# Weights laid out in memory by eight keys: whole rows for the loads, 512-byte pieces for the stores

## The chip, the core and the metric

The kernel runs on one core of a Trainium2 chip. The metric is the time of one execution on the device, in microseconds, as the median of several runs. One further execution was profiled; every duration below comes from it.

## What is computed

One inference step of a small trunk layer: modulation, latent attention and retention in parallel, an output projection, and then an expert layer (PEER) on 9 tiles of 128 tokens. Only the expert layer matters here. Each token picks 16 of 16384 experts for each of 8 heads, an expert being a pair of keys (i, j) with i and j below 128:

```python
eidx = jnp.take_along_axis(cidx, sel, axis=-1)
g = jax.nn.softmax(top_s, axis=-1).astype(xb.dtype)
act = jax.nn.gelu(jnp.einsum('thkd,td->thk', u_table[eidx], xb), approximate=False)
return jnp.einsum('thk,thkd->td', g * act, v_table[eidx])
```

## The kernel before

The first three tiles of tokens (the sparse ones) gather their experts' rows. The other six are done densely, in two groups of 384 tokens: for each of the 128 values of key j, TensorE multiplies the tokens by all 128 experts (i, j) of `u` (lines 2835, 2836 and 2839, in high and low halves, into `p_a`), ScalarE applies gelu, VectorE multiplies by the token's weight for that expert (line 2689, `w_ring`), and TensorE multiplies by the experts of `v` into `p_y` (line 2853). One value of j is a step.

The weights of a group are a tensor over 128 i (the partitions), 128 j and 384 tokens. Class `WeightSteps` makes them, four tokens at a time: VectorE writes one-hot rows (`vector`), TensorE multiplies them (`tensor`, line 2252), ScalarE copies the product from its bank to `wt` (`scalar`, line 2260). Four such calls fill a block of 16 tokens, of which `wt` holds two, and `store` (lines 2262 to 2267) writes a block, 1 MB, to `w_dram` in memory ("weights_spill" in the rows). The store first waits for every store before it (line 2265 counts it), then frees a half of `wt` for ScalarE, then waits for ScalarE's four copies, then issues.

The work is written out by hand for each engine, and each engine and each queue runs its list in order:

- The first group's 24 blocks are made ahead of the steps, in a stage of their own. SyncE stores them, and issues between two stores a load of `u_ahead` (buffers named `rows<-in_uT` in the rows), of `hs` (`x1g<-h_spill`) or of the first u and v. TensorE meanwhile multiplies ahead for the last 16 steps (line 2810, `down_ahead`) and ScalarE sends the results to memory (`act_ahead`).
- The second group's 24 blocks are made during steps 0 to 95 of the first group, one block every four steps; GpSimd stores them.
- The weights come back by eight keys j and all 384 tokens, 1.5 MB at a time, into one of the two halves of `w_ring` (`load_w`, line 2574, issued by GpSimd once every eight steps). The very first is loaded in four parts while the last blocks are still being made (line 2601).
- Behind these on GpSimd's queue stand the gathers of the sparse tiles (line 2583, 768 of 512 KB), whose rows VectorE uses between its other work (lines 2702 and 2714).

In memory a block was `[128 i, 128 j, 16 tokens]`, so that a store wrote 8 KB in one piece per row, and a load of eight keys read 24 pieces of 512 bytes per row, one from each block, 1 MB apart.

Of the kernel before, what the change touches and what calls it, by code (L numbers as in the profile page):

```python
# [6 lines left out]
F32 = mybir.dt.float32  # L7
# [9 lines left out]
P = 128  # L17
# [20 lines left out]
N_KEYS = 128  # L38
N_EXPERTS = N_KEYS * N_KEYS
GROUP = 3  # L40
SPARSE = 3
DENSE_AT = SPARSE * P
DENSE = T - DENSE_AT
BLOCK = 16
NEG = -3.0e38
SHARE_UNIT = 2.0 ** 14
LATE_PIECES = 16
# [1229 lines left out]
def wait_count(eng, sem, count):  # L1277

    if not isinstance(count, int) or count > 0:
        eng.wait_ge(sem, count)  # L1280
# [380 lines left out]
def stage_scores(nc, sem, m, keep, a):  # L1661
# [71 lines left out]
    with nc.Block() as block:  # L1733
# [328 lines left out]
        def _(dve):  # L2062
# [77 lines left out]
            def sixteen_best(x, rest, values, where, groups):  # L2140
# [7 lines left out]
                for g in groups:  # L2148
                    last = nc.vector.match_replace(rest[:, g, :], values[:, g, 0:8], x[:, g, :], NEG)
                link(last)  # L2150
# [51 lines left out]
class WeightSteps:  # L2202
# [7 lines left out]
    STEPS = GROUP * P // B  # L2210
    PER_BLOCK = BLOCK // B
    LEAD = 2

    def __init__(self, nc, sem, m, keep, iota):
# [6 lines left out]
        self.iota = iota.rearrange("p (k b) -> p k b", b=self.IN)  # L2221
        self.wt = m.sb("wt", [P, 2, N_KEYS, BLOCK])
        self.iota_full, self.equal_full, self.hot_full, self.pw_full, self.pw_read, self.wt_free, self.stored, self.stored_next = (
# [38 lines left out]
    def store(self, eng, block, stored, ahead=0):  # L2262

        wait_count(eng, stored, (block - ahead) * 16)
        eng.sem_inc(self.wt_free, 1)
        eng.wait_ge(self.pw_read, block * self.PER_BLOCK + (self.PER_BLOCK + self.LEAD))
        eng.dma_start(self.keep.w_dram[block], self.wt[:, block % 2]).then_inc(stored, 16)


def stage_experts(nc, sem, m, keep, a):  # L2270
# [15 lines left out]
    x1 = [m.sb(f"x1g{i}", [P, D]) for i in range(GROUP)]  # L2286
    w = WeightSteps(nc, sem, m, keep, keep.pairsT[:, 2, DENSE_AT:DENSE_AT + N_KEYS * WeightSteps.IN // 2].bitcast(F16))
    BLOCKS = w.STEPS // w.PER_BLOCK
    JC = 8
    TB = GT // BLOCK  # L2290
    w_ring = m.sb("w_ring", [P, 2, TB, JC, BLOCK])
    rows = [[m.sb(f"rows{s}{i}", [P, D]) for i in range(SLOTS)] for s in range(SPARSE)]
# [31 lines left out]
    h_in, u_in, v_in, w_in, w_early = sem("h_in"), pair("u_in"), pair("v_in"), sem("w_load"), sem("w_early")  # L2324
# [11 lines left out]
    def out_rows(t):  # L2336
        return a["out"][0][0] if t == 0 else a["out"][1][0, (t - 1) * P:t * P, :]
# [21 lines left out]
    def parts_after(g, j):  # L2359

        whole = J - AHEAD * g
        total = J + 2 * whole
        passed = j + 1 + 2 * min(j + 1, whole)
        return min(SPARSE * J, -(-SPARSE * J * passed // total) + SPARSE * ((j >= 4) + (j >= 8)))
# [56 lines left out]
    with nc.Block() as block:  # L2421
# [143 lines left out]
        @block.gpsimd  # L2565
        def _(pool):
            CHUNKS = J // JC

            def load_w(g, c):

                n = c + g * CHUNKS
                wait_count(pool, w_in, n * 16)
                wait_count(pool, g_full, (n - 1) * JC + 1)
                pool.dma_start(w_ring[:, n % 2], keep.w_dram[g * TB:(g + 1) * TB, :, c * JC:(c + 1) * JC, :].rearrange("b i j t -> i b j t")).then_inc(w_in, 16)

            def gather(g, j, paced=lambda s: None):

                n = g * J + j
                for s in range(SPARSE):
                    paced(s)  # L2580
                    wait_count(pool, rows_used, (n - SLOTS) * SPARSE + s + 1)
                    at = bass.IndirectOffsetOnAxis(ap=keep.experts[:, s, j:j + 1].bitcast(U32), axis=0)
                    pool.indirect_dma_start(rows[s][n % SLOTS][:], None, (keep.u_rows, v_rows)[g], at).then_inc(rows_in[s][n % SLOTS], 16)  # L2583

            def load_x1(g):
                for i in range(GROUP):
                    wait_count(pool, y_out[0][i], 16 * g)
                    pool.dma_start(x1[i][:], keep.x1_dram[SPARSE + g * GROUP + i]).then_inc(x1_in[i], 16)

            pool.dma_start(h_ahead, keep.h2_dram[:, :, DENSE_AT + GT:DENSE_AT + 2 * GT]).then_inc(h_ahead_in, 16)  # L2590
            for i, part in enumerate(H_PARTS):
                pool.wait_ge(w.stored, 16 * (H_BEHIND + i))
                wait_count(pool, h_in, 16 * i)
                pool.dma_start(h_lo[:, part, :].bitcast(F32), keep.h2_dram[:, part, DENSE_AT:DENSE_AT + GT]).then_inc(h_in, 16)
            pool.wait_ge(idx_done, 2)
            for g in range(GROUPS):
                if g == 0:
                    gather(g, 0, lambda s: pool.wait_ge(w.stored, 16 * (ROWS_BEHIND + s)))
                    for blocks_in, behind in W_BEHIND:
                        pool.wait_ge(w.stored, 16 * behind)  # L2600
                        pool.dma_start(w_ring[:, 0, blocks_in], keep.w_dram[blocks_in, :, 0:JC, :].rearrange("b i j t -> i b j t")).then_inc(w_in if behind == BLOCKS else w_early, 16)
                    pool.wait_ge(ahead_full, STEPPED)
                    gather(g, 1)
                else:
                    gather(g, 0)
                    gather(g, 1)
                    load_w(g, 0)
                load_w(g, 1)
                if g == 0:
                    pool.wait_ge(cols_turned, SPARSE)  # L2610
                    load_x1(0)
                asked = SLOTS
                for j in range(J):
                    enough = min(parts_after(g, j) // SPARSE + SLOTS, J)
                    for n in range(asked, enough):
                        gather(g, n)
                    asked = max(asked, enough)
                    if g < GROUPS - 1 and j < w.STEPS and j % w.PER_BLOCK == w.PER_BLOCK - 1:
                        w.store(pool, j // w.PER_BLOCK + BLOCKS, w.stored_next, BLOCKS)
                    if j % JC == JC - 1 and j // JC + 2 < CHUNKS:  # L2620
                        load_w(g, j // JC + 2)
                    if g == 0 and j == w.STEPS + 8:
                        pool.wait_ge(w.stored_next, 16 * BLOCKS)
                        pool.dma_start(h_next, keep.h2_dram[:, :, DENSE_AT + GT:DENSE_AT + 2 * GT]).then_inc(h_in, 16)
                    if g and j == 4:
                        for i in range(GROUP):
                            pool.wait_ge(y_full, i + 1)
                            pool.dma_start(out_rows(SPARSE + i), x1[i][:]).then_inc(y_out[0][i], 16)
                    if g and j == 16:
                        load_x1(1)  # L2630
            for s in range(SPARSE):
                pool.wait_ge(rows_used, (2 * J - 2) * SPARSE + s + 1)
                pool.dma_start(x1_sparse[s], keep.x1_dram[s]).then_inc(xs_in[s], 16)

        @block.vector
        def _(dve):
# [43 lines left out]
            def weigh(n, j, s):  # L2680
# [6 lines left out]
                dve.wait_ge(w_in, (n // JC) * 16 + 16)  # L2687
                three = lambda x: x.rearrange("p (b t) -> p b t", t=BLOCK)
                nc.vector.tensor_mul(three(g_all[s]), three(act_g[s]), w_ring[:, (n // JC) % 2, :, n % JC, :]).then_inc(g_full, 1)  # L2689
# [194 lines left out]
def build(nc, a, debug=None):  # L2884
    with ExitStack() as stack:
        top = Mem(nc, stack)
        keep = Keep()
# [23 lines left out]
        keep.z_dram = nc.dram_tensor("z_spill", [TILES, P, Z_RET], F32).ap()  # L2911
        keep.x1_dram = nc.dram_tensor("x1_spill", [TILES, P, D], F32).ap()
        keep.h2_dram = nc.dram_tensor("h2_spill", [P, KD, T], F32).ap()
        keep.w_dram = nc.dram_tensor("weights_spill", [DENSE // BLOCK, P, N_KEYS, BLOCK], F32).ap()
        keep.u_rows = nc.dram_tensor("u_rows", [N_EXPERTS, D], F32).ap()
        keep.w_in_in = [stack.enter_context(nc.semaphore(f"w_in_in{c}")) for c in range(2)]

# [52 lines left out]
        keep.h_rows = top.sb("h_rows", [P, SPARSE, D])  # L2970
        keep.index, keep.parts = (top.sb(x, [P, 2, DENSE], F16)[:] for x in ("index", "parts"))
        run(stage_experts)


# [41 lines left out]
```

## Time and profile before

| | |
|---|---|
| median of 3 runs | 3575.25 us |
| the runs | 3573.58, 3575.25, 3584.92 us |
| the profiled execution's own time | 3585.65 us |
| its span, first to last instruction | 3583.9 us |
| TensorE busy | 3444.2 us, 96% |
| VectorE busy | 2941.8 us, 82% |
| ScalarE busy | 1391.3 us, 39% |
| GpSimd busy | 1483.9 us, 41% |
| moved by DMA | 1047.91 MB, mean 292 GB/s |

The busy shares are means over stages with different limits; the stage with the first group's weights is 137 us of the 3584, the steps about 2100. A DMA's time to landing runs from its issue to its last semaphore write. Rows name engines as PE (TensorE), DVE (VectorE), ACT (ScalarE), POOL (GpSimd) and SP (SyncE); a q behind the name is the engine's queue of instructions. The DMA engines serve three queues here: q1 is SyncE's, q10 ScalarE's, q0 GpSimd's.

### The profile page before, as it was taken

The page shows a single profiled execution, that of the slowest core. Times are in us where ns is not written, and L with a number is a line of the kernel's source. Part 1 is how long each engine was busy: PE and PEld are TensorE (multiplying, and loading weights), DVE is VectorE, ACT ScalarE, POOL GpSimd, SP SyncE. Part 2 cuts the span into 40 slices and gives each one's busy share as a digit, 9 for nine tenths or more (in the row PEclk, how much of TensorE's full clock was granted, in tenths as well). Part 3 has the DMA queues.
Part 4 walks back from the last instruction along what each step waited for, and adds up shares of the span by engine and source line. Part 5 has one row for each costly group of instructions (what it writes and reads, how often), then busy time and mean ns, then how long its engine had stood idle before and what let it go on. Part 6 is the DMA issues. An engine that isn't in the chain of part 4 may idle for free.

```text
span 3583.9 us, 55129 instructions
## 1 busy us (share of the span) xinstructions
PE 3444.2 (96%) x18146; PEld 2870.1 (80%) x18146; DVE 2941.8 (82%) x5762; ACT 1391.3 (39%) x2125; POOL 1483.9 (41%) x1121
## 2 busy tenths in 40 slices
PE   7899989988999989999999999999999999999998
PEld 2899869876444456788888998899988999999987
DVE  8455678854688899799999999988888988988988
ACT  7411464462122238434444444433333333333332
POOL 3233020052322210254444444454466776666761
PEclk9999999999999989999999999999999999999999
DMA  8599429856311138999999999999999999999997
GB/s 310 205 359 354 157 101 320 300 215 211 132 35 35 65 119 322 325 355 348 346 354 352 339 354 351 350 357 367 311 344 376 379 364 369 374 355 363 374 364 286
DMA packets 399666, 1047.91 MB, mean 292 GB/s; under 512 B 32106, under 2 KB 185550, under 8 KB 390194
## 3 DMA queue, kind: packets, MB, share of 16 engines
q0 software_dynamic: 134416, 505.99, 39.1%
q1 hardware_dynamic: 213612, 478.03, 36.6%
q10 hardware_dynamic: 51512, 62.42, 5.0%
q8 instruction: 53, 0.87, 0.1%
q14 instruction: 73, 0.60, 0.1%
HBM read 892.52 MB, written 153.80 MB: 292 GB/s over the span
## 4 chain that ended last, share of the span: by engine, by line
PE 55%; DMA 4%; DVE 2%; issue 1%; ACT 0%; POOL 0%; ACTq 0%; DVEq 0%; SPq 0%; POOLq 0%
PE p_y L2853 26%; PE p_a L2836 9%; PE p_a L2839 8%; PE p_a L2835 8%; PE pw L2252 1%; DMA weights_spill<-wt 1%; DMA pairsT<-act_ahead 1%; PE p_y L2810 1%; DMA rows<-in_v,pairsT 1%; DVE rows L2702 0%; DMA x1g<-h_spill 0%; DMA rows<-u_rows,pairsT 0%; DVE h_rows L2714 0%; POOL rows L2583 0%; ACT wt L2260 0%
## 5 line engine op out<-in xcount | busy, mean ns | idle before, releaser
L2583 POOL DMA_INDIRECT rows<-u_rows,pairsT x384 | 492.2, 1282 | 580.8 <-DVE pairsT L2702 531.9
L2583 POOL DMA_INDIRECT rows<-in_v,pairsT x384 | 591.6, 1541 | 333.2 <-DVE h_rows L2714 248.2
L2835 PE MATMUL p_a<-h_hi,u_hi 128*128 128x384 f32 x1856 | 624.0, 336 | 4.9 <-ACT pairsT L2531 4.0
L2836 PE MATMUL p_a<-h_lo,u_hi 128*128 128x384 f32 x1856 | 627.3, 338 | 0.0
L2714 DVE SCALAR_TENSOR_TENSOR h_rows<-rows,pairsT,h_rows 128x1024 f32<-128x1024 f32 x381 | 476.8, 1280 | 53.8 <-DMA rows<-in_v,pairsT 53.6
L2702 DVE CUSTOM_DVE_ANT_0 rows<-rows,h_rows 128x1024 f32<-128x1024 f32 x384 | 459.2, 1220 | 22.1 <-DMA rows<-u_rows,pairsT 22.0
L2853 PE MATMUL p_y<-v_hi,g_hi 128*128 128x512 f32 x1464 | 464.8, 399 | 4.7 <-ACT g_hi L2537 4.7
L2853 PE MATMUL p_y<-v_lo,g_hi 128*128 128x512 f32 x1464 | 454.6, 391 | 0.0
L2853 PE MATMUL p_y<-v_hi,g_lo 128*128 128x512 f32 x1464 | 373.2, 390 | 3.0 <-DVE g_lo L2696 3.0
L2839 PE MATMUL p_a<-h_hi,u_lo 128*128 128x384 f32 x1856 | 361.1, 335 | 8.3 <-DVE u_lo L2662 8.3
L2835 PEld LDWEIGHTS p_a<-h_hi,u_hi 128*128 128x128 f32 x1856 | 350.1, 189 | 15.4 <-issue 5.3
L2836 PEld LDWEIGHTS p_a<-h_lo,u_hi 128*128 128x128 f32 x1856 | 349.7, 188 | 8.9
L2537 ACT ACTIVATE g_hi<-pairsT 128x384 fp32r<-128x384 f32 x256 | 134.7, 526 | 568.3 <-DVE pairsT L2689 563.8
L2524 ACT ACTIVATE v_hi<-v_raw 128x1024 fp32r<-128x1024 f32 x244 | 257.4, 1055 | 243.9 <-PE p_y L2853 241.6
L2662 DVE TENSOR_TENSOR u_lo<-u_raw,u_hi 128x1024 fp32r<-128x1024 f32 x232 | 283.2, 1221 | 64.9 <-ACT u_hi L2506 64.9
L2839 PEld LDWEIGHTS p_a<-h_hi,u_lo 128*128 128x128 f32 x1856 | 325.9, 188 | 9.3 <-DVE u_lo L2662 9.2
L2853 PEld LDWEIGHTS p_y<-v_lo,g_hi 128*128 128x128 f32 x1464 | 275.1, 188 | 62.5
L2853 PEld LDWEIGHTS p_y<-v_hi,g_lo 128*128 128x128 f32 x1464 | 275.5, 188 | 60.6 <-DVE g_lo L2696 3.4
L2678 DVE TENSOR_TENSOR v_lo<-v_raw,v_hi 128x1024 fp32r<-128x1024 f32 x244 | 297.8, 1221 | 9.3 <-ACT v_hi L2524 6.4
L2853 PEld LDWEIGHTS p_y<-v_hi,g_hi 128*128 128x128 f32 x1464 | 265.6, 188 | 49.1 <-ACT g_hi L2537 6.4
L1904 PE MATMUL psc<-wc,hs 128*128 128x512 f32 x576 | 251.5, 595 | 0.0
L2260 ACT ACTIVATE wt<-pw 128x512 f32 (+1 forms) x144 | 157.3, 1092 | 237.7 <-PE pw L2252 223.8
(386 smaller groups left out, 6013.7 us busy)
## 6 DMA issues: line engine op xcount, KB each, us to landing
v_raw<-in_v SPq DMA_DIRECT2D x244, 512.0 KB, 6.6
u_raw<-in_uT SPq DMA_DIRECT2D x232, 512.0 KB, 7.3
w_ring<-weights_spill POOLq DMA_DIRECT2D x31, 1536.0 KB, 14.5
wada<-in_w_ada SPq DMA_DIRECT2D x48, 512.0 KB, 7.0
u_rows<-pairsT ACTq DMA_DIRECT2D x48, 512.0 KB, 6.8
key_cols<-in_uT SPq DMA_DIRECT2D x48, 512.0 KB, 7.5
u_rows<-key_rows SPq DMA_DIRECT2D x48, 512.0 KB, 5.7
weights_spill<-wt SPq DMA_DIRECT2D x24, 1024.0 KB, 5.1
```

What stands on the lines that cost most here:

```text
L1904: last = nc.tensor.matmul(psc[:, 4 * b:4 * b + 4, :], hs[:, k, :], wc[:, k, 4 * b:4 * b + 4, :], start=k == 0, stop=k == KD - 1)
L2260: self.nc.scalar.activation(out.rearrange("p j b -> p b j"), banks[s % len(banks)], ACT.Copy, scale=1.0 / SHARE_UNIT).then_inc(self.pw_rea ...
L2524: nc.scalar.activation(hi, raw, ACT.Copy).then_inc(vhi_full, 1)
L2583: pool.indirect_dma_start(rows[s][n % SLOTS][:], None, (keep.u_rows, v_rows)[g], at).then_inc(rows_in[s][n % SLOTS], 16)
L2662: nc.vector.tensor_sub(u_lo[s][:], u_raw[s][:], u_hi[s][:].bitcast(F32)).then_inc(ulo_full, 1)
L2678: nc.vector.tensor_sub(lo, raw, hi.bitcast(F32)).then_inc(vlo_full, 1)
L2702: nc.vector.tensor_tensor_reduce(out=slot[:], in0=slot[:], in1=keep.h_rows[:, s, :], op0=ALU.mult, op1=ALU.add, scale=1.0, scalar=0.0, acc ...
L2714: nc.vector.scalar_tensor_tensor(out=total, in0=slot[:], scalar=share, in1=total, op0=ALU.mult, op1=ALU.add).then_inc(rows_used, 1)
L2835: nc.tensor.matmul(p_a[:, 0:GT], u_hi[s][:, k, :], h_hi[:, k, :], start=k == 0, stop=False)
L2836: nc.tensor.matmul(p_a[:, 0:GT], u_hi[s][:, k, :], h_lo[:, k, :], start=False, stop=False)
L2839: last = nc.tensor.matmul(p_a[:, 0:GT], u_lo[s][:, k, :], h_hi[:, k, :], start=False, stop=k == KD - 1)
L2853: last = nc.tensor.matmul(p_y[i][:, half, :], part[s][:, i * P:(i + 1) * P], vv[:, half * 512:(half + 1) * 512], start=begin, stop=stop)
```

## The change

The tensor in memory gets another order: group, chunk of eight keys, i, block, key in the chunk, token. A store takes the same block from `wt` and writes it as 16 pieces of 512 bytes per row i, one for each chunk, 1.5 MB apart. A load of a chunk reads 12 KB in one piece per row; the four early parts read 4 KB or 2 KB in one piece per row. No instruction is added, removed or moved on any engine: only the shapes of the 48 stores and the 35 loads differ.

```diff
+W_KEYS = 8
...
-        eng.dma_start(self.keep.w_dram[block], self.wt[:, block % 2]).then_inc(stored, 16)
+        group, b = divmod(block, GROUP * P // BLOCK)
+        rows = self.keep.w_dram[group][:, :, b].rearrange("c i j t -> i c j t")
+        eng.dma_start(rows, self.wt[:, block % 2].rearrange("i (c j) t -> i c j t", j=W_KEYS)).then_inc(stored, 16)
...
-                pool.dma_start(w_ring[:, n % 2], keep.w_dram[g * TB:(g + 1) * TB, :, c * JC:(c + 1) * JC, :].rearrange("b i j t -> i b j t")).then_inc(w_in, 16)
+                pool.dma_start(w_ring[:, n % 2], keep.w_dram[g, c]).then_inc(w_in, 16)
...
-                        pool.dma_start(w_ring[:, 0, blocks_in], keep.w_dram[blocks_in, :, 0:JC, :].rearrange("b i j t -> i b j t")).then_inc(w_in if behind == BLOCKS else w_early, 16)
+                        pool.dma_start(w_ring[:, 0, blocks_in], keep.w_dram[0, 0][:, blocks_in]).then_inc(w_in if behind == BLOCKS else w_early, 16)
...
-        keep.w_dram = nc.dram_tensor("weights_spill", [DENSE // BLOCK, P, N_KEYS, BLOCK], F32).ap()
+        keep.w_dram = nc.dram_tensor("weights_spill", [DENSE // (GROUP * P), N_KEYS // W_KEYS, P, GROUP * P // BLOCK, W_KEYS, BLOCK], F32).ap()
```

## Rows read from the trace of the kernel before

**Rows 1.** Busy by stretch: us; PE, PEld, DVE, ACT, POOL (instructions); clock, DMA, GB/s.
```profile
1389.00:1442.00 53.00, 51.44 (x393) 33.31 (x392) 51.00 (x149) 42.76 (x49) 7.78 (x8) 1.00 0.98 355
...
1600.00:2345.00 745.00, 745.00 (x4218) 669.89 (x4217) 682.02 (x1181) 322.78 (x423) 339.99 (x288) 1.00 0.96 348
...
2620.00:3500.00 880.00, 867.52 (x4352) 785.52 (x4351) 783.55 (x789) 312.47 (x417) 590.03 (x382) 1.00 0.98 367
...
1577.00:1584.00 7.00, 6.41 (x20) 5.86 (x20) 5.94 (x12) 0.00 (x0) 4.82 (x3) 0.54 1.02 397
```

**Rows 2.** What SyncE's queue waited for, 1315 to 1475 us: total, times, longest.
```profile
SPq L2265 <- DMA weights_spill<-wt: 101.2, 23, 6.6
SPq L2267 <- ACT wt L2260: 23.6, 12, 13.3
```

**Rows 3.** The 24 stores on SyncE: issue in ns; then landing in us, min/median/max.
```profile
L2267 SPq DMA_DIRECT2D weights_spill<-wt x24: 319/326/332, 1326.8 to 1463.7; - x24
...
DMA to landing us min/median/max: 4.4/5.1/6.9
```

**Rows 4.** Chain that ended last, 1388 to 1443 us: start, us, what.
```profile
by line: DMA weights_spill<-wt 85.4%; ACT wt L2260 8.3%; issue 5.6%; ACT pairsT L2495 0.6%; ACTq L2497 0.6%; SPq L2265 0.3%; ACTq L1280 0.0%; ACTq L2258 0.0%
...
1406.81 5.19 DMA weights_spill<-wt
...
1412.09 6.93 DMA weights_spill<-wt
```

**Rows 5.** The tensor h_spill on SyncE's queue, 880 to 1240 us.
```profile
L1754 SPq DMA_DIRECT2D h_spill<-hs x9: 540/561/602, 888.9 to 1231.2; - x9
...
DMA to landing us min/median/max: 3.7/3.8/8.8
```

**Rows 6.** The tensor x_spill on SyncE's queue, the same stretch.
```profile
L1752 SPq DMA_DIRECT2D x_spill<-x x8: 350/352/371, 903.4 to 1214.5; - x8
...
DMA to landing us min/median/max: 2.6/2.7/2.7
```

**Rows 7.** DMA, 1103.3 to 1107 us; a queue's packets, MB, share of 16 engines.
```profile
DMA packets 1080, 0.69 MB, mean 186 GB/s; under 512 B 16, under 2 KB 1040, under 8 KB 1080
...
q1 hardware_dynamic: 1080, 0.69, 70.7%
```

**Rows 8.** DMA, 1326.8 to 1330.4 us; issues with KB and us to landing.
```profile
q1 hardware_dynamic: 121, 0.99, 82.9%
...
rows<-in_uT SPq DMA_DIRECT2D x1, 512.0 KB, 5.7
```

**Rows 9.** Between the weights' stage and the steps: timeline of POOL, then the chain.
```profile
1468.82 0.75 POOL L2601 DMA_DIRECT2D w_ring<-weights_spill  x1 [20.27 <-DMA weights_spill<-wt]
...
1469.53 7.12 DMA act_ahead<-pairsT
```

**Rows 10.** All DMA issues: KB each, median us to landing.
```profile
x1g<-h_spill SPq DMA_DIRECT2D x3, 512.0 KB, 7.2
...
w_ring<-weights_spill POOLq DMA_DIRECT2D x2, 256.0 KB, 6.7
```

**Rows 11.** DMA, 1482 to 1485.5 us, while a load of weights ran.
```profile
q0 software_dynamic: 240, 0.98, 99.3%
```

**Rows 12.** DMA, 1488.1 to 1489.9 us, while rows of 4 KB were loaded.
```profile
q0 software_dynamic: 194, 0.73, 101.1%
```

**Rows 13.** The tensor weights_spill: time of an issue on GpSimd, ns min/median/max.
```profile
L2574 POOL DMA_DIRECT2D w_ring<-weights_spill x31: 1455/1498/1512, 1475.6 to 3510.9; - x31
...
L2267 POOL DMA_DIRECT2D weights_spill<-wt x24: 579/592/607, 1521.1 to 2340.2; - x24
```

**Rows 14.** Who waited for whom, 2650 to 2720 us: total, times, longest.
```profile
DVE h_rows L2714 <- DMA rows<-in_v,pairsT: 9.6, 5, 5.4
...
PE p_a L2839 <- DVE u_lo L2662: 8.3, 2, 7.3
```

**Rows 15.** The same view, 1570 to 1590 us.
```profile
PE p_y L2853 <- DVE g_lo L2696: 3.0, 1, 3.0
```

More of the change, by code:

```diff
@@ L2288, in stage_experts @@
     BLOCKS = w.STEPS // w.PER_BLOCK
-    JC = 8
+    JC = W_KEYS
     TB = GT // BLOCK
```

## The prediction, made before the changed kernel ran

> **What bounds the kernel now.** I read the busy shares by stretch first, then what the store's queue waits for, then the chain that ended last, because the change touches only transfers and a transfer matters where something waits for it.
>
> The kernel writes and reads the weights in two very different places. From 1600 to 2345 us, the first group's steps, TensorE is busy 745.00 of 745.00 us, and from 2620 to 3500 us 867.52 of 880, while the DMA engines are 96% and 98% busy [rows 1]. There TensorE is the bound, and a transfer counts only where it makes TensorE wait. From about 1327 to 1464 us lies the stage that makes the first group's weights: 24 blocks, each stored by SyncE. Its middle, 1389 to 1442 us, shows TensorE 51.44, VectorE 51.00 of 53 us, and the DMA engines at 0.98 [rows 1]: three things are near their limit at once. The order of waits settles it. SyncE waited 101.2 us, 23 times, for the previous store to land, and 23.6 us for ScalarE to fill the next block; the longest of these, 13.3 us, is the wait ahead of the first store [rows 2]. So between the first store (1326.8) and the last (1463.7) only 23.6 - 13.3 = 10.3 us passed in which the data and not the previous store was late. The stores take 4.4 to 6.9 us to land, median 5.1 [rows 3]. The chain of work shows the same: from 1388 to 1443 us 85.4% of it is store after store, the next one issued 0.09 us after the one before has landed (1412.09 behind 1406.81 + 5.19) [rows 4]. The code says why: `store` waits for all earlier stores before it hands ScalarE the other half of `wt`, and one store is in flight at a time. This is the one place where a microsecond of a store is a microsecond of the kernel.
>
> **The stores of the first stage (the term that decides).** 23 intervals take 136.9 us; without the 10.3 us of slack they are 126.6 us, 5.50 us each: a landing and a restart. If a store lands d later, the stage needs 23 x (5.50 + d) us, which is 23d - 10.3 us more than now, and nothing below d = 0.45. Nothing hides it: ScalarE has two halves of `wt`, both then full or in flight, and TensorE and VectorE are let on by ScalarE's reads of the banks. Everything on SyncE's queue behind the store (the loads of `u_ahead`, which feed the matmuls ahead of the steps, and the first u and v) moves along.
>
> What is d? The trace holds a pair that differs only in pieces. `h_spill<-hs` writes 512 KB in 1024 pieces of 512 bytes and lands in 3.8 us; its issue takes 561 ns [rows 5]. `x_spill<-x` writes 512 KB in 128 pieces of 4 KB, lands in 2.7 us, and its issue takes 352 ns [rows 6]. So 1.1 us more for 1024 pieces. A second way goes by the packets: around one `h_spill` store 1080 packets ran, 1024 of them the pieces, 16 semaphore writes and 40 packets of the load behind it, and took 70.7% of 16 engines in 3.7 us [rows 7], 41.9 us; less 40 x 163 ns (below) that is 35 ns a piece. So SyncE's queue does not join pieces. A store of today is 8 KB packets, 121 in 82.9% of 16 x 3.6 us [rows 8], 395 ns each, or 25 ns per 512 bytes. The change makes 2048 pieces of each store: 2048 x 10 ns / 16 = 1.3 us, and the longer issue adds about 0.2. I take d = 1.5. The low end is the 1.1 us of the pair as it stands, the high end twice that, 2.2 us, since there are twice the pieces. So the stage grows by 24.2 us (15.0 to 40.3).
>
> The Trainium skill (DMA: Bandwidth & Descriptors, Specifications) puts the smallest piece at line rate at 512 bytes, by which d would be 0 and the term 0; the same page (Why small descriptors are slow) charges some 3 cycles on top of 16 for a 512-byte piece, 19%, which as an estimate on 3.2 us of packets is d = 0.6 and a term of 3.5 us. [Rows 7, 8] speak against both: 35 against 25 ns.
>
> **The end of that stage.** After the last store lands, GpSimd issues the last piece of the first weights (1468.82) [rows 9]; such a piece takes 6.7 us [rows 10], so it is there at about 1475.5, and ScalarE waits for another transfer, `act_ahead<-pairsT`, from 1469.53 for 7.12 us anyway [rows 9]. A store 1.5 us later uses up the 1.2 us of margin, and the piece, now 2 KB per row instead of four pieces, gives some back. I put 0, at most 1 us.
>
> **The loads of the steps.** 31 loads of 1.5 MB are now 24 pieces of 512 bytes per row and become one of 12 KB. GpSimd's queue joins pieces to 4 KB packets: while only a w load ran, 240 packets took 99.3% of 16 x 3.5 us, 232 ns each [rows 11]; while 4 KB rows ran, 0.73 MB, 178 packets, took 101.1% of 16 x 1.8 us, 163 ns each [rows 12]. A load is 384 packets, so it gives the engines 384 x 69 / 16 ns = 1.7 us back, and GpSimd's issue falls from 1498 ns to about the 592 ns that 128 pieces cost [rows 13]. A gather that is issued behind a load lands some 2.6 us sooner.
>
> The 24 stores on GpSimd go the other way: between 592 ns (128 pieces) and 1498 ns (3072) [rows 13] 2048 pieces lie at 1.2 us, and 256 packets at 232 ns are 3.7 us of the engines where 128 at 326 to 395 ns are 2.6 to 3.2. So each costs 0.6 us of issue and 0.5 to 1.1 us of transfer. Behind them wait gathers, behind these VectorE's dots, and behind these TensorE; in the stretch with 745 of 745 us of matmul nothing of it arrives [rows 1]. If that cover were gone it would be at most 24 x 1.7 = 41 us.
>
> What can be won is what TensorE waits today because of late gathers: 8.3 us around 2695, behind a VectorE that waited up to 5.4 us for rows of `in_v` [rows 14], and 3.0 us at 1577 [rows 15]. Behind the second the granted clock was 0.54 from 1577 to 1584, so near the lower of its two levels, 1.2 GHz [rows 1]. The first becomes 2.6 us shorter. The second has a store and a load ahead of its gathers: 2.6 less, 1.1 to 1.7 more, so 1.0 shorter. Together -3.6 us, with the clock's dip left.
>
> **Sum.** The profiled execution took 3585.65 us (span 3583.9, 1.75 around it). 3585.65 + 24.2 + 0 - 3.6 = 3606. It stands 10.4 us over the median of the runs, so the median becomes 3596 us. A measurement here tells about 0.3% (11 us) from no change.
>
> **Rivals.**
> (a) The small pieces cost little (d below 1.1): the store's 8 KB packets of today are already held up by memory, so shorter ones may fit into the same time. For it speaks 395 ns against 326 ns, twice the 4 KB packet; against it the pair of rows 5 and 6. At d = 0.45 or less it gives 3575.25 - 3.6 = 3572, at 0.7 3577. Chance 0.22 with all that ends within 0.3%.
> (b) The other side: faster. The gathers behind the shorter loads come soon enough that TensorE never waits in the steps. That is worth 8.3 + 3.0 us and the dip (7 us at 0.54, 3.2 us; twice that if the longer wait has one too), 18 us, and 3557 if the stores cost nothing. It decides only if the stage grows by less than 6 us, which is d below 0.7, and the profile's waits recur in the unprofiled runs. DMA at 98% in the steps speaks for it, TensorE at 867.5 of 880 for its small size. Chance 0.06.
> (c) Much slower. Small pieces suffer beside other traffic: `x1g<-h_spill`, 512 KB in 1024 pieces behind a store, lands in 7.2 us [rows 10], a load of 512 KB in 4 KB pieces behind a store in 5.7 [rows 8]: 1.5 us for 1024 pieces, d = 3.0 for 2048. The pieces of a row now lie 1.5 MB apart too. The stage grows by 58.7 us: 3630. TensorE, with 5.8 us of work per block (0.97 of today's 136.9 / 23 = 5.95), would then idle 2.7 us in 8.5, close to the 3.0 us that it had idled when the clock stood at 0.54. Chance 0.12.
> The forecast itself (d from 1.1 to 2.2; 3587 to 3612) has 0.60.
>
> **Numbers.** The range takes the forecast's own range, the upper part of (a) down to d = 0.7, and the lower part of (c): 3577 to 3616. Slower by over 0.3% (above 3586): 0.60 + 0.12. Within: 0.22. Faster: 0.06.
>
> **What would show it.** In the profile after, the 24 stores on SyncE land in a median of 6.4 to 6.8 us instead of 5.1 and their issue takes about 0.8 us; SyncE's wait for ScalarE between stores is nearly gone; from the first store to the last it is 160 us, not 137; TensorE's share in that stage falls from 0.97 to 0.83 with the clock still at 1. The w loads take about 0.6 us to issue and land some 2 us sooner. VectorE waits less for `in_v` rows. I am wrong if the stores land below 5.6 us, or if the stage grows and the steps shrink by as much, which needs TensorE waits that the trace of before doesn't have.

## The result, and the profile after

| | before | changed |
|---|---|---|
| median | 3581.41 us (7 runs) | 3594.84 us (7 runs) |
| range of the runs | 3573.58 to 3584.92 | 3590.25 to 3601.26 |
| ratio | | 1.004, 95% interval 1.0029 to 1.0051 |
| span of the profiled execution | 3583.9 us | 3593.4 us |
| first to last store of the first stage | 136.9 us | 157.5 us |
| last of these stores to the end | 2120.2 us | 2114.6 us |

The changed kernel is 0.4% slower. Between the two profiled executions there are 9.5 us: 20.6 more in the stage that makes the first group's weights, 5.6 less behind it, and 5.5 less ahead of the first store, where nothing was changed and executions simply differ.

What SyncE's queue waited for in that stage of the changed kernel, as in [rows 2]; lines have moved by three:

```profile
SPq L2266 <- DMA weights_spill<-wt: 90.2, 23, 9.2
SPq L2270 <- ACT wt L2261: 18.4, 7, 13.4
```

The stores on SyncE, as in [rows 3]:

```profile
L2270 SPq DMA_DIRECT2D weights_spill<-wt x24: 359/374/385, 1321.3 to 1478.8; - x24
...
DMA to landing us min/median/max: 5.3/5.8/9.6
```

The median landing has gone from 5.1 to 5.8 us and the longest from 6.9 to 9.6. The wait for ScalarE between stores (without the first one's 13.4) is 5.0 us where it was 10.3: the chain of stores sets nearly every interval. What a store costs without other traffic shows at the first one of the changed kernel. In the 5.2 us behind its issue (1321.3 to 1326.5) SyncE's queue moved

```profile
q1 hardware_dynamic: 2059, 1.08, 77.8%
```

That is 77.8% of 16 engines for 5.2 us, or 31 ns a packet, where 512 bytes of an 8 KB packet took 25 ns in [rows 8]. For 2048 pieces on 16 engines the difference is 0.8 us a store. The chain that ended last, 1380 to 1445 us, as in [rows 4]:

```profile
by line: DMA weights_spill<-wt 98.6%; PE p_y L2813 4.1%; ACT wt L2261 3.3%; PE p_a L2253 1.3%; issue 1.2%; PE pw L2253 1.0%; SPq L2266 0.2%; ACTq L2259 0.0%
...
1374.70 5.60 DMA weights_spill<-wt
...
1386.21 8.12 DMA weights_spill<-wt
...
1414.72 9.57 DMA weights_spill<-wt
...
1424.37 5.68 DMA weights_spill<-wt
...
1430.13 9.32 DMA weights_spill<-wt
```

The shares add up to more than 100%, since the first store of this chain begins at 1374.70, ahead of the stretch. Without it the stores are some 58.8 of the 65 us, 90%.

Busy times by stretch, the columns of [rows 1]. First the whole stage of the kernel before:

```profile
1326.80:1463.70 136.90, 131.80 (x998) 87.18 (x997) 127.26 (x364) 108.75 (x118) 9.47 (x10) 0.97 0.88 314
```

then of the changed kernel: that stage, a piece of it, and the second and third stretch of [rows 1], moved to where the same work now lies:

```profile
1321.30:1478.80 157.50, 140.06 (x1003) 91.38 (x1001) 129.76 (x365) 107.89 (x118) 7.53 (x10) 0.93 0.90 273
...
1424.00:1431.00 7.00, 5.49 (x29) 3.88 (x30) 2.86 (x8) 5.07 (x6) 1.72 (x2) 0.51 0.79 231
...
1613.00:2358.00 745.00, 745.00 (x4217) 669.92 (x4216) 682.24 (x1182) 323.07 (x423) 348.01 (x288) 1.00 0.95 349
...
2628.00:3509.00 881.00, 872.36 (x4373) 789.93 (x4372) 790.12 (x793) 315.18 (x419) 577.40 (x384) 1.00 0.97 369
```

In the stage TensorE has the same work and shows 8 us more of it, since its clock was at the lower level, 1.2 GHz, for part of the time: from 1424 to 1431 us the granted clock is 0.51, after TensorE had waited 3.6 us for ScalarE. The steps of the first group are as full of matmul as before, 745 of 745 us. In those of the second group TensorE's waits have shrunk, from 12.5 of 880 us (880 - 867.52) to 8.6 of 881. The part of [rows 13] and of [rows 14], after:

```profile
L2577 POOL DMA_DIRECT2D w_ring<-weights_spill x31: 561/592/612, 1491.4 to 3520.0; - x31
...
L2270 POOL DMA_DIRECT2D weights_spill<-wt x24: 1208/1229/1250, 1535.4 to 2352.8; - x24
```

```profile
DVE h_rows L2717 <- DMA rows<-in_v,pairsT: 8.6, 7, 3.4
...
PE p_a L2842 <- DVE u_lo L2665: 6.3, 2, 5.3
```

### The profile page after: what moved, and what is told of

Same layout as the page of the kernel before. It is cut to its first block, busy times and chain, and to the rows that moved or that the text cites. A ratio compares the mean times of both kernels' runs of the same rounds, so it can differ in the third digit from the quotient of the medians.

```text
span 3593.4 us, 55129 instructions
## 1 busy us (share of the span) xinstructions
PE 3445.0 (96%) x18146; PEld 2868.0 (80%) x18146; DVE 2947.2 (82%) x5762; ACT 1391.3 (39%) x2125; POOL 1465.6 (41%) x1121
## 4 chain that ended last, share of the span: by engine, by line
PE 54%; DMA 6%; DVE 2%; issue 1%; POOL 0%; ACT 0%; SPq 0%; DVEq 0%; ACTq 0%
PE p_y L2856 26%; PE p_a L2839 9%; PE p_a L2842 8%; PE p_a L2838 8%; DMA weights_spill<-wt 3%; PE pw L2253 1%; DMA pairsT<-act_ahead 1%; DMA rows<-in_v,pairsT 1%; PE p_y L2813 0%; DVE rows L2705 0%; DMA x1g<-h_spill 0%; POOL rows L2586 0%; DMA rows<-u_rows,pairsT 0%; DVE h_rows L2717 0%; DVE u_lo L2665 0%
## 5 line engine op out<-in xcount | busy, mean ns | idle before, releaser
L2705 DVE CUSTOM_DVE_ANT_0 rows<-rows,h_rows 128x1024 f32<-128x1024 f32 x384 | 458.8, 1220 | 10.3 <-DMA rows<-u_rows,pairsT 10.3
L2681 DVE TENSOR_TENSOR v_lo<-v_raw,v_hi 128x1024 fp32r<-128x1024 f32 x244 | 298.1, 1222 | 12.5 <-ACT v_hi L2527 7.0
## 6 DMA issues: line engine op xcount, KB each, us to landing
w_ring<-weights_spill POOLq DMA_DIRECT2D x31, 1536.0 KB, 11.8
```

Of the source, the lines that this page charges most:

```text
L2681: nc.vector.tensor_sub(lo, raw, hi.bitcast(F32)).then_inc(vlo_full, 1)
L2705: nc.vector.tensor_tensor_reduce(out=slot[:], in0=slot[:], in1=keep.h_rows[:, s, :], op0=ALU.mult, op1=ALU.add, scale=1.0, scalar=0.0, acc ...
```

## The experiments

My theory: the loss lies in SyncE's 24 stores of the first stage and there alone; it is the price of small pieces times a chain in which one store waits for the landing of the last; the loads of the steps give a few microseconds back. Rivals: GpSimd's small stores cost in the steps; the distance between the pieces and not their size matters; the DMA engines are simply full.

### Half of the change each (late_only, early_only)

```diff
+        if group == OLD_GROUP:
+            eng.dma_start(self.keep.w_blocks[b], self.wt[:, block % 2]).then_inc(stored, 16)
+            return
```

The group `OLD_GROUP` keeps the order of before, in a tensor of its own, and its loads are those of before: group 0 in late_only, group 1 in early_only.

> The first group's weights keep the old block order (stores of 8 KB pieces by SyncE, loads of 512-byte pieces), only the second group's use the new one (stores of 512-byte pieces by GpSimd during the first group's steps, loads of 12 KB by GpSimd in the second group's steps). My theory: the whole loss is the serial chain of SyncE's stores in the first stage, so that stage is back at 137 us from first store to last (changed kernel: 157.5), and the steps keep most of their gain of 4.7 us: 0.1% under the kernel before, some 3577 against 3581, so no difference that is clear or a slightly faster kernel. Rival 1 (the small pieces cost in the steps too, by GpSimd's 24 stores): slower than before by 3 us or more, with TensorE waiting longer between 1500 and 2600 us. Rival 2 (the loss is in the loads or at the change to the steps): the stage's length does not matter and the time stays near 3595.

> The other half: only the first group's weights use the new order. My theory: the stage takes the 157 us of the changed kernel, the first group's steps gain a little from their 12 KB loads, the second group's nothing; 3597, ratio to before 1.0045. Rival 1 (GpSimd's small stores cost in the steps): this kernel is faster than the changed one by 3 us or more. Rival 2: under 3585, if the first stage is not where the time goes.

late_only: 3578.53 us, ratio to before 0.999 (0.9982 to 0.9999). early_only: 3600.45 us, 1.0053 (1.0039 to 1.0068). The stores on SyncE, of late_only and of early_only:

```profile
L2271 SPq DMA_DIRECT2D weights_blocks<-wt x24: 319/326/334, 1324.3 to 1460.1; - x24
...
DMA to landing us min/median/max: 4.3/5.1/7.2
```

```profile
L2274 SPq DMA_DIRECT2D weights_spill<-wt x24: 359/374/386, 1321.8 to 1478.3; - x24
...
DMA to landing us min/median/max: 5.3/6.0/9.7
```

The stage takes 135.8 us with old stores and 156.5 with new ones. With the first group's new stores goes the whole loss. early_only is 3.5 us over its forecast of 3597 and 5.6 us slower than the changed kernel, not 3 us faster as rival 1 (GpSimd's small stores cost in the steps) would have it. The gain sits mostly in the second group's steps. They begin with VectorE's rounding of the next tokens; that row for the kernel before, for the changed one, for late_only and for early_only:

```profile
L2780 DVE CAST h_hi<-wt x1: 1753/1753/1753, 2589.4 to 2589.4; 128x3072 fp32r<-128x3072 f32 x1
```

```profile
L2783 DVE CAST h_hi<-wt x1: 1754/1754/1754, 2601.8 to 2601.8; 128x3072 fp32r<-128x3072 f32 x1
```

```profile
L2787 DVE CAST h_hi<-wt x1: 1756/1756/1756, 2588.7 to 2588.7; 128x3072 fp32r<-128x3072 f32 x1
```

```profile
L2787 DVE CAST h_hi<-wt x1: 1755/1755/1755, 2602.4 to 2602.4; 128x3072 fp32r<-128x3072 f32 x1
```

Taken from the spans (3583.9, 3593.4, 3578.4, 3599.6) that leaves 994.5 and 997.2 us for the second group with loads of 512-byte pieces and 991.6 and 989.7 with loads of 12 KB: 3 to 7 us less. The other kernels below agree: this part is 995 to 997 us in keys16, two_before and three_before, which load 512-byte pieces there, and 990 to 993 us in the seven that load larger ones.

The part between the last store of the stage and that row is 1125.7, 1123.0, 1128.6 and 1124.1 us in the same order. With 12 KB loads it is 1.6 us shorter (before against early_only) or 5.6 (late_only against the changed kernel). With GpSimd's small stores it is 2.9 us longer (late_only against before) or 1.1 us shorter (the changed kernel against early_only), which is no effect that single executions can show.

### The distance between the pieces (near)

```diff
-[DENSE // (GROUP * P), N_KEYS // W_KEYS, P, GROUP * P // BLOCK, W_KEYS, BLOCK]
+[DENSE // (GROUP * P), P, N_KEYS // W_KEYS, GROUP * P // BLOCK, W_KEYS, BLOCK]
```

> The changed kernel with the same 16 pieces of 512 bytes per row and store, but a row's 16 pieces lie 12 KB apart in memory (order: group, i, chunk, block, key, token) instead of 1.5 MB, and a load still reads 12 KB in one piece per row, the rows now 192 KB apart. My theory (the number of pieces sets the price): stores on SyncE land in a median of 5.8 us, the stage takes 155 to 160 us, the time is that of the changed kernel within 0.15%. Rival (the distance sets the price): stores land near 5.1 us, the stage near 140 us, the time near 3580.

3594.68 us, 1.0038 (1.0024 to 1.0051), that is the changed kernel's time. Its stores on SyncE:

```profile
L2270 SPq DMA_DIRECT2D weights_spill<-wt x24: 512/516/545, 1317.2 to 1479.5; - x24
...
DMA to landing us min/median/max: 5.4/6.3/8.2
```

The stage takes 162.3 us, 2 us beyond what I had written, with a longer issue (0.52 us) and a median of 6.3 us where I had 5.8. The time is as forecast. Pieces 12 KB apart are no cheaper than pieces 1.5 MB apart, so a large distance is not what costs.

### The size of the pieces (keys4, keys16)

```diff
-W_KEYS = 8
+W_KEYS = 4
```

or 16, with the load still eight keys: for keys4 two pieces of 6 KB per row into a ring laid out by four keys, for keys16 24 pieces of 512 bytes.

> The changed kernel with chunks of four keys: a store writes 32 pieces of 256 bytes per row, 4096 pieces in all, and a load reads two pieces of 6 KB per row into a ring laid out by four keys. Going from 8 KB pieces to 2048 pieces of 512 bytes added 0.7 us to the median landing and about 0.9 us to each interval of the stage. My theory (each piece is a packet with a fixed part, and the chain is serial): with twice the pieces the median landing rises to 6.7 to 8 us and the stage to 175 to 200 us, the time to 3615 to 3640. Rival (the engines are held up by memory and not by packets): landing under 6.2 us and the time under 3605.

> Chunks of sixteen keys: a store writes 8 pieces of 1 KB per row, and a load of eight keys reads 24 pieces of 512 bytes per row as in the kernel before. It gives the third point beside 8 KB (stage 137 us), 512 bytes (157) and 256 bytes (185). Packets of 1 KB take 46 to 49 ns elsewhere in these traces, 1024 of them 3.0 us of 16 engines, no more than the 128 packets of 8 KB do today at 395 ns (3.2 us). By that the stage would be 137 to 142 us and the time that of the kernel before. If instead each added piece costs the same, half of the loss remains: stage 145 to 149 us, time 3588 to 3592.

keys4: 3619.93 us, 1.0101 (1.0081 to 1.012). keys16: 3588.07 us, 1.002 (1.001 to 1.003). The stores of keys4, then of keys16:

```profile
L2270 SPq DMA_DIRECT2D weights_spill<-wt x24: 359/374/386, 1322.7 to 1507.7; - x24
...
DMA to landing us min/median/max: 6.4/7.7/10.5
```

```profile
L2270 SPq DMA_DIRECT2D weights_spill<-wt x24: 359/374/383, 1315.5 to 1460.3; - x24
...
DMA to landing us min/median/max: 5.0/5.6/8.8
```

| piece | pieces per row | median landing | stage | time |
|---|---|---|---|---|
| 8 KB (before) | 1 | 5.1 us | 136.9 us | 3579.7 to 3581.5 |
| 1 KB (keys16) | 8 | 5.6 | 144.8 | 3588.1 |
| 512 bytes (changed) | 16 | 5.8 | 157.5 | 3594.8 |
| 256 bytes (keys4) | 32 | 7.7 | 185.0 | 3619.9 |

keys4 came out as the theory had it. keys16 did not come out by my packet times, which had the stage at 137 to 142 us. It came close to the other forecast, half of the loss for half of the pieces: the time of 3588.07 is within it, the stage of 144.8 just below its 145. What was wrong in the first forecast is the price of a packet, which I had taken from other transfers at 46 to 49 ns. The first store of keys16, in the 4.8 us behind its issue:

```profile
q1 hardware_dynamic: 1058, 1.13, 80.4%
```

That is 80.4% of 16 engines for 4.8 us. Less 19 packets of 4 KB at 163 ns, which belong to the load behind, the 1024 pieces took 57 ns each. That is 3.7 us of 16 engines for a store where the 8 KB packets of before are 3.2, and 0.5 us is what the median landing rose by. The cost is not the same for each added piece, though: keys16 adds 7 pieces per row and 7.9 us of stage, the changed kernel 15 and 20.6, keys4 31 and 48.1, which is 1.1, 1.4 and 1.6 us for each. That keys16's profiled span of 3583.1 is low for its stage has one part in a first store at 1315.5 us, 11 us ahead of that of before.

### Two stores in flight with two places (two_after, two_before, two_late)

```diff
-        wait_count(eng, stored, (block - ahead) * 16)
-        eng.sem_inc(self.wt_free, 1)
+        if not ahead:
+            self.landed(eng, block - 2)
+            landing = self.landings[block % 2]
...
-            act.sem_inc(w.wt_free, 1)
+            act.sem_inc(w.wt_free, 2)
```

`landed` waits for that block's own semaphore, then counts it in `stored` and frees its half of `wt`.

> The changed kernel, but SyncE issues a block's store as soon as ScalarE has filled it, with up to two stores in flight (one semaphore for each half of wt; ScalarE gets a half back when the store two blocks ago has landed). My theory (the small pieces cost because one store waits for the landing of the one before): the chain is cut, the stage from first to last store falls from 157.5 us to 140 to 147, bounded by the DMA engines' own work (0.90 of 157.5 = 142 us) and TensorE's (132), and the time falls by 10 to 18 us to about 3580. Rival (the DMA engines' throughput with 2048 small packets per store is what bounds the stage): landings grow by as much as the overlap gives and the stage stays above 152 us.

> The kernel before with the same two stores in flight. TensorE has 132 us of work in a stage of 137 us and the DMA engines 121, so there is little to win: the stage at 132 to 136 us, the time lower by 1 to 5 us, which the measurement can hardly tell from none. If the chain of stores was not what held the stage in the kernel before, there is no change at all.

> The first group's weights in the old block order with two stores in flight, the second group's in the new order: the sum of the two gains, 2 to 5 us from each: 3572 to 3577, ratio to before 0.998 to 0.999. It should be the fastest of all, and by little.

All three were slower than the kernels that they were made from: two_after 3609.36 us (1.0077, 1.0061 to 1.0093), two_before 3590.1 (1.0022, 1.0012 to 1.0033), two_late 3588.92 (1.0017, 1.0007 to 1.0027). The forecasts failed, and by something that I had not seen in my own edit. Who waited for whom in two_after, 1320 to 1500 us:

```profile
ACT wt L2262 <- SPq L2271: 51.1, 18, 5.2
PE pw L2254 <- ACT wt L2262: 28.6, 15, 4.4
```

The stage took 174.0 us in two_after (1322.2 to 1496.2) and 143.9 in two_before. The landings are off the path there, but SyncE frees a half only after it has issued the next store and the loads behind it, so that ScalarE is no longer a block ahead. In two_before, with 8 KB pieces, this order alone costs 7.0 us of stage (136.9 to 143.9); in two_after it costs 16.5, and there the issues behind the stores are slow. SyncE's queue of the changed kernel around the store at 1430 us:

```profile
1430.13 0.36 SPq L2270 DMA_DIRECT2D weights_spill<-wt  x1
1430.55 3.97 SPq L2430 DMA_DIRECT2D rows<-in_uT  x1
1439.54 6.79 SPq L2270 DMA_DIRECT2D weights_spill<-wt  x2
```

The store's own issue takes 0.36 us, and the next instruction 3.97 instead of the 0.43 us of the same load in the kernel before. So one wait was exchanged for another, and the runs say nothing on the chain of landings. That the slow issues make up the difference between 7.0 and 16.5 us was not tested by itself.

### Three places for a block (three_after, three_before, three_late)

```diff
+    def place(self, block):
+        if not isinstance(block, int) or block >= 24:
+            return self.wt[:, block % 2]
+        if block > 20:
+            return self.wt[:, (0, 1, 0)[block - 21]]
+        return self.third if block % 3 == 2 else self.wt[:, block % 3]
...
+        elif block > 1:
+            self.landed(eng, block - 2)
+            if block != 22:
+                eng.sem_inc(self.wt_free, 1)
...
-            act.sem_inc(w.wt_free, 1)
+            act.sem_inc(w.wt_free, 3)
```

`third` is the memory of the gate rows, which are loaded behind the last store. SyncE now waits for the store before the last, ahead of the next issue.

> The run with two stores in flight (two_after) made things worse, since there SyncE freed a half of wt only after it had issued the next store and the loads behind it: ScalarE then waited 51 us for SyncE. Here the changed kernel gets a third place for a block (in the memory that the gate rows fill later), SyncE waits for the store before the last, and ScalarE is always one block ahead. My theory: now the chain of landings is really cut; the stage falls from 157.5 us to 140 to 148, TensorE's and the DMA engines' own work, and the time to 3578 to 3586. Rival (the DMA engines cannot take 2048 small packets per store any faster): the landings lengthen to 9 us or more and the stage stays at 152 to 160 us, the time at 3590 or more.

> The kernel before with the third place. Its stage has 132 us of TensorE work in 137, so at most 5 us are to be won: stage 132 to 136 us, time 3577 to 3581. It separates the gain of the third place from what it takes off the small pieces: if it gains as much as the changed kernel does (over 10 us), the chain had nothing to do with the size of the pieces.

> Third place, old block order for the first group, new order for the second: the sum of two small gains, stage 132 to 136 us and steps 2 to 5 us shorter than before: 3573 to 3579, ratio 0.998 to 0.999. It should be the fastest of all.

three_after: 3580.02 us, ratio to before 0.9994 (0.9983 to 1.0006). three_before: 3577.41, 0.999 (0.998 to 0.9999). three_late: 3577.38, 0.9988 (0.9977 to 0.9998). The 17 stores of three_after from `wt` (7 more come from the third place), what SyncE waited for, and the stage as a whole, of three_after and then of three_before:

```profile
L2290 SPq DMA_DIRECT2D weights_spill<-wt x17: 359/377/2477, 1328.0 to 1466.4; - x17
...
DMA to landing us min/median/max: 5.7/8.1/11.6
```

```profile
SPq L2290 <- ACT wt L2270: 52.6, 15, 13.4
SPq L2275 <- DMA weights_spill<-wt: 20.1, 7, 5.2
```

```profile
1328.00:1466.40 138.40, 131.88 (x997) 87.43 (x995) 127.39 (x364) 109.53 (x117) 7.79 (x10) 0.97 0.99 311
```

```profile
1320.10:1451.70 131.60, 130.22 (x998) 87.01 (x996) 126.78 (x364) 109.54 (x117) 8.98 (x10) 0.98 0.91 327
```

With the same small pieces, and landings of 8.1 us in the median, the stage falls from 157.5 to 138.4 us: SyncE waits 20.1 us for landings instead of 90.2, and TensorE is busy 131.88 of 138.40 us. The kernel before, given the same place, goes from 136.9 to 131.6 us in its stage (first store 1320.1, last 1451.7). Both stages are a little below their forecasts (140 to 148 and 132 to 136). So the new order loses 20.6 us with two places and 6.8 with three: 13.8 us, two thirds of the loss, come from the chain. In whole times it loses 13.4 us with two places and 2.6 with three. The 6.8 that stay fit the DMA engines as the bound: their share is 0.99 of 138.4 us, 137 us of work, where three_before has 0.91 of 131.6, 120 us, and is held by TensorE (130.22 of 131.60). This was not tested further. three_late has a stage of 132.3 us and the 12 KB loads of the second group, and is 0.1% under the kernel before, as late_only and three_before are; these three cannot be told apart.

### The gathers beside the stores (gathers_late)

```diff
-    H_BEHIND, ROWS_BEHIND = 11, 15
+    H_BEHIND, ROWS_BEHIND = 11, 22
```

> The changed kernel with the three early gathers of rows (512 KB each on GpSimd's queue) held back until stores 22 to 24 have landed, and the early loads of weights behind them. Its stage is what is looked at; what comes behind it starts later and costs some microseconds. Store 17 (the 17th, issued at 1430 us) lands in 9.3 us in the changed kernel and in 6.0 us in the kernel before, where the traffic beside it was nearly the same. Theory A (a queue of 512-byte packets gets one packet for each packet of 4 KB of another queue, so it loses most beside GpSimd's transfers): that landing falls below 7 us, and stores 17 and 19 together lose 3 us or more. Theory B (the long landings come from the store's own queue, where two loads were issued ahead of it): it stays at 8.5 us or more.

One run: 3590.69 us, profiled span 3588.9. SyncE's queue at the same store:

```profile
1425.75 0.36 SPq L2270 DMA_DIRECT2D weights_spill<-wt  x1
1426.16 1.70 SPq L2430 DMA_DIRECT2D rows<-in_uT  x1
1432.36 6.73 SPq L2270 DMA_DIRECT2D weights_spill<-wt  x2
```

From this store to the next it is 6.6 us, where it was 9.4 in the changed kernel with a gather of 512 KB beside it, and the load's issue is 1.70 instead of 3.97 us. It lands in 6.2 us instead of 9.3, and store 19 in 5.7 instead of 8.0. The stage is 150.5 us (1317.5 to 1468.0), 7.0 less. Theory A holds for these two stores: with small pieces they suffer from another queue's large packets, by 3.1 and 2.3 us. That it is one packet for one packet was only argued. The longest landing stays (9.7 us); it lies at 1410 us beside `h_lo` and behind two loads of its own queue, and was not taken apart. Theory B may have its part as well, though no run separates it. The store of the changed kernel at 1386.21 stands behind two loads of its own queue, and GpSimd's first transfer of the stage is issued only at 1394.63. It lands in 8.1 us, where the same store (1389.10) landed in 5.8 before, with two loads ahead of it and 192 KB of ScalarE's beside it both times. The issue behind it is the slowest of the stage:

```profile
1386.63 4.70 SPq L2430 DMA_DIRECT2D rows<-in_uT  x1
```

## Why the prediction was right, and where its steps were off

- **What bounds.** Right. The stage of SyncE's stores is the only place where the change cost, shown by late_only and early_only. The chain of landings is the reason for 13.8 of the 20.6 us, shown by three_after; the other 6.8 stay without it.
- **The time: right in part by luck.** I forecast a median of 3596 us and it is 3594.84. But the change was forecast as 24.2 - 3.6 = 20.6 us, and by the medians it is 13.4. The sum started from 3575.25, the median of three runs of the kernel before, and the median of its seven runs is 3581.41: 6.2 us that made up for most of what was too much in the change.
- **23 x d - 10.3.** The serial chain was right, both numbers of the sum were off, and they partly cancelled. By the measure of the prediction d is (157.5 - 5.0) / 23 - 5.50 = 1.1 us, the low end of the pair and not the 1.5 taken; the median landing is 5.8 us and not 6.4 to 6.8. The slack did not vanish: 5.0 of 10.3 us stayed, most of it in the first six intervals, where the chain runs through the loads of `hs` (`x1g<-h_spill`) and TensorE rather than through the stores. 23 x 1.13 is 26 us more of landings, of which the slack took up 5.3. That leaves the 20.6 us measured, but for rounding, where 24.2 were forecast from 34.5 and 10.3.
- **What d is made of.** I took 35 ns a piece from the stores of `h_spill`; the changed store's own packets took 31. That alone gives 0.8 us instead of 1.3, near the rise of the least landing (0.9 us, 4.4 to 5.3) and of the median (0.7). The rest of the mean of 1.1 comes from stores with other traffic about them: the longest landing rose by 2.7 us. Holding back GpSimd's gathers gave back 7.0 us of the stage in one run. That was the mechanism of rival (c), at a smaller size. The prediction's second estimate by packets, d = 0.6, was near the price of a store alone, but its term of 3.5 us leaves out this traffic and the slack that stayed.
- **The doubling** of the pair's 1.1 us for twice the pieces, the high end of the range, did not happen: 2048 pieces cost no more over 128 of 8 KB than 1024 over 128 of 4 KB.
- **The issue.** I forecast 0.8 us. It is 0.374 us; the rest shows at the instruction behind the store, 1.5 to 4.7 us for a load that took 0.43 in the median.
- **The clock.** "Still at 1" was wrong: the granted clock was 0.93 over the stage, with dips behind the longest waits, and 0.97 before. So TensorE's share fell to 0.89 (140.06 of 157.50) and not to 0.83, which is what the 131.8 us of before would give. TensorE was not the bound there. Little time hangs on the clock: the chain passes through slow matmuls at 1440.7 to 1444.8 us, where SyncE then waits 0.6 us for ScalarE.
- **The end of the stage: 0.** Right within a microsecond. VectorE's first multiply with `w_ring` starts 13.6 us behind the last store before (1477.25) and 12.7 behind it after (1491.51), and what ScalarE waited for is `act_ahead<-pairsT` both times. So 0.8 of the 5.6 us won behind the last store lie here.
- **The loads: -3.6.** Right in sign, and near in size: 5.6 us less behind the last store, of which 2.9 in the second group. The loads land in a median of 11.8 us instead of 14.5, where some 2 us were forecast. VectorE's longest wait for `in_v` rows fell from 5.4 to 3.4 us, TensorE's of 7.3 to 5.3: 2.0 us, where 2.6 were forecast. The wait of 3.0 us at 1577 became 2.5, where 1.0 less was forecast. GpSimd's issues are 592 ns for a load (592 forecast) and 1229 for a store (1.2 us forecast).
- **Rival (a)**, small pieces cost little: fallen, but narrowly. By the intervals d is 1.13 and the rival ended at 1.1; a change of 13.4 us is little more than the 11 that I had named as the least that a measurement tells from none. **Rival (b)**, faster: its gain exists, 3 to 7 us in the second group, and late_only shows it alone. **The rule of the Trainium skill** (DMA: Bandwidth & Descriptors, Specifications) that 512 bytes is enough for line rate: against it stand 0.7 us more per median landing and the row of keys16, where even 1 KB costs 8 us of stage.

## What to carry to other kernels

When a layout must have small pieces on one side, ask which side has a chain of single transfers that wait for each other, and which has a queue with room: here each load landed 2.7 us sooner with whole rows and each store only 1.1 us later with small pieces, but the store was the one waited for. If small pieces must stay there, break the chain with one more buffer rather than reorder two: the third place took 19 us off the stage, the reordering with two places added 16.5. And count in an issuing queue what stands behind a transfer of many pieces, not only the transfer.

## What the runs showed of the hardware that I had not expected

- A DMA of 2048 pieces from SyncE takes 0.37 us to issue, about as long as one of 128 (0.33). The next DMA on that queue then takes 1.5 to 4.7 us where it took 0.43 in the median. Behind the same store it was 4.0 us with GpSimd's gather beside it and 1.7 without; it was 4.7 us where two loads of the same queue stood ahead of the store.
- On SyncE's queue each piece of these stores is a packet of its own: 2059 packets ran with one store of 2048 pieces. On GpSimd's queue a DMA of 128 pieces takes 0.59 us to issue, with pieces of 12 KB (the loads after) as with pieces of 8 KB (the stores before).
- 1 KB pieces were not free: median landing 5.6 us against 5.1 for 8 KB, and 57 ns a packet, or 29 ns per 512 bytes, against 25.
